# Joined SwiGLU products of 512 columns, a reordered beginning, and moved weight splits in a two-block transformer kernel

## The reference

```python
def swiglu(x, w13, w2):
    g, u = jnp.split(x @ w13, 2, axis=-1)
    return (jax.nn.silu(g) * u) @ w2
...
        if kind == 0:
            mix = gated_deltanet(h, a_w_in[j], a_conv[j], a_a_log[j], a_dt_bias[j], a_norm_g[j], a_w_out[j])
        elif kind == 1:
            mix = moba_attention(h, b_w_qkv[j], b_w_out[j])
...
        h = layer_norm(DEEPNORM_ALPHA * h + mix, ln1_g[i], ln1_b[i])
        h = layer_norm(DEEPNORM_ALPHA * h + swiglu(h, f_w13[i], f_w2[i]), ln2_g[i], ln2_b[i])
...
def half_ffn(h, shift, scale, gate, g_pre, g_post, w13, w2):
    u = modulate(rmsnorm(h, g_pre), shift, scale)
    return h + 0.5 * gate * rmsnorm(swiglu_2(u, w13, w2), g_post)
```

## Time and profile before

| | before |
|---|---|
| three timed runs | 1744.97, 1747.71 (median), 1751.12 us |
| profiled execution, its own time | 1749.66 us |
| its span | 1747.9 us |
| mean granted TensorE clock | 0.984 |
| busy share PE, PEld, DVE, ACT, POOL | 96%, 88%, 54%, 44%, 9% |
| read from HBM | 303.69 MB, 174 GB/s over the span |

### The profile page before, as it was taken

How to read it: one execution, slowest core, us unless ns; L and a number is a source line. 1 busy time by engine, 2 the same in 40 slices (tenths; PEclk the granted TensorE clock), 3 DMA queues, 4 the chain that set the end, 5 groups by cost and what they waited for, 6 DMA issues and landing times.

```text
span 1747.9 us, 27671 instructions
## 1 busy us (share of the span) xinstructions
PE 1680.7 (96%) x11886; PEld 1539.4 (88%) x11886; DVE 948.0 (54%) x1085; ACT 764.5 (44%) x979; POOL 165.4 (9%) x170
## 2 busy tenths in 40 slices
PE   7999999999899899999999999999999999989998
PEld 6996787999777689988999899989889999879997
DVE  4664236554535565556655565556766364665543
ACT  4454333444325534433444354444655354444432
POOL 0113420000000100001000130012100020020000
PEclk8999999999999999999999999999999999999999
DMA  7553238665556786655765566645445242676652
GB/s 230 146 180 133 98 121 252 183 191 186 202 175 235 243 248 188 189 193 169 196 179 184 180 191 174 188 169 183 154 141 154 69 138 92 199 224 180 177 187 95
DMA packets 329168, 306.54 MB, mean 175 GB/s; under 512 B 11953, under 2 KB 286934, under 8 KB 328918
## 3 DMA queue, kind: packets, MB, share of 16 engines
q1 hardware_dynamic: 324246, 296.19, 55.3%
q10 hardware_dynamic: 4528, 7.54, 1.3%
q0 software_dynamic: 272, 1.05, 0.2%
HBM read 303.69 MB, written 1.05 MB: 174 GB/s over the span
## 4 chain that ended last, share of the span: by engine, by line
PE 87%; DVE 6%; ACT 3%; DMA 2%; issue 1%; POOL 1%; SPq 0%; DVEq 0%; POOLq 0%; ACTq 0%
PE ps L412 49%; PE ps L436 17%; PE ps L455 8%; ACT whi L383 2%; PE ps L473 1%; DVE wlo L389 1%; PE ps L1178 1%; PE ps L1194 1%; PE ps L1798 1%; PE ps L594 1%; DMA raw<-in_b_w_qkv 1%; PE ps L2396 1%; PE ps L2295 1%; DVE x L708 1%; DVE small L663 0%
## 5 line engine op out<-in xcount | busy, mean ns | idle before, releaser
L389 DVE TENSOR_TENSOR wlo<-raw,whi 128x2048 fp32r<-128x2048 f32 x247 | 567.7, 2300 | 408.6 <-ACT whi L383 408.5
L412 PE MATMUL ps<-ah,whi 128*128 128x256 f32 x2368 | 678.1, 286 | 7.1 <-DVE wlo L389 7.1
L412 PE MATMUL ps<-ah,wlo 128*128 128x256 f32 x2368 | 672.8, 284 | 0.0
L412 PE MATMUL ps<-al,whi 128*128 128x256 f32 x2368 | 672.8, 284 | 0.0
L383 ACT CAST whi<-raw 128x2048 fp32r<-128x2048 f32 x247 | 470.0, 1905 | 246.6 <-PE ps L436 157.1
L412 PEld LDWEIGHTS ps<-ah,whi 128*128 128x128 f32 x2368 | 457.5, 193 | 10.1 <-issue 7.1
L412 PEld LDWEIGHTS ps<-al,whi 128*128 128x128 f32 x2368 | 457.4, 193 | 1.8 <-issue 1.4
L412 PEld LDWEIGHTS ps<-ah,wlo 128*128 128x128 f32 x2368 | 457.2, 193 | 0.0
L764 ACT ACTIVATE f_sig<-ps 128x256 f32<-128x256 f32 x110 | 42.1, 383 | 359.2 <-PE ps L412 345.3
L436 PE MATMUL ps<-whi,fh 128*128 128x512 f32 x440 | 171.6, 390 | 0.0
L436 PE MATMUL ps<-wlo,fh 128*128 128x512 f32 x440 | 171.3, 389 | 0.0
(11 more groups left out here) (360 smaller groups left out, 1642.2 us busy)
## 6 DMA issues: line engine op xcount, KB each, us to landing
raw<-in_f_w SPq DMA_DIRECT2D x132, 512.0 KB, 4.6
raw<-in_w_a SPq DMA_DIRECT2D x132, 512.0 KB, 4.6
raw<-in_w_ada SPq DMA_DIRECT2D x72, 512.0 KB, 4.6
raw<-in_w_in SPq DMA_DIRECT2D x68, 512.0 KB, 4.6
raw<-in_w_b SPq DMA_DIRECT2D x66, 512.0 KB, 4.7
raw<-in_a_w_in SPq DMA_DIRECT2D x32, 512.0 KB, 5.2
raw<-in_b_w_qkv SPq DMA_DIRECT2D x24, 512.0 KB, 5.8
raw<-in_a_w_out SPq DMA_DIRECT2D x8, 512.0 KB, 4.0
```

The lines of the kernel that those rows point to most:

```text
L389: dve.tensor_tensor(wlo[:, c % RING, :], raw[:, r % RING, :], whi[:, c % RING, :].bitcast(F32), ALU.subtract).then_inc(S("lo_ready"), 1)
L412: last = pe.matmul(out_ap, a, b, start=(i == 0), stop=(i == n - 1))
```

## The change

It does four things.

1. The up segments become kind "U". For each block and `k` there is one product of 512 columns, wh x [ah | al] (`ah` and `al` are now the two halves of one tile `a_split`), and one of 256, wl x ah. The sums xh·wh + xh·wl stand in the left half of a bank and xl·wh in the right half; a chunk takes two banks. ACT copies both right halves out, DVE adds them to the left halves, and Silu and the product follow (`gate_sum`, `summed`).
2. At the beginning the two tiles of x are loaded first on two queues, the turn goes in the order 0, 2, 1, 3, chunk 0 is split in two halves, PE gets six products of a constant around the turn (`warm_pe`), the gates are computed as 16 rows (24 products of 256 columns, a copy and two transposes), `params_pe` moves from behind chunk 0 to behind chunk 1, and the sums and norms move two chunks later.
3. On DVE, the splits of up0's, m_qkv's, up1's and up4's chunk 1 move from in front of the row pass to behind the turn (turns 1, 2, 3 and 8).
4. The row pass in front of up2 is spread over DVE's work on up2's chunks 0 to 3.

```diff
-        Segment("up0", KF, "B", gate_up(A["f_w13"][0]), evicted="hid"),
+        Segment("up0", KF, "U", gate_up(A["f_w13"][0]), evicted="summed"),
...
+    UP_BANKS = ((0, 1), (2, 4), (5, 6))
...
+        sp.dma_start(x0[:, 1, :], A["x"][0, P:T, :]).then_inc(S("x_in1"), 16)
...
+    def start_cuts_act(act):
+        act.wait_ge(*S("landed0", 32))
+        act.copy(whi[:, 0, 0:HALF], raw[:, 0, 0:HALF]).then_inc(S("hi_first"), 1)
+        act.copy(whi[:, 0, HALF:CHUNK], raw[:, 0, HALF:CHUNK]).then_inc(S("hi_ready"), 1)
+        for c in range(1, RING):
+            cut_hi(act, c)
+    def start_cuts_dve(dve):
+        for name, done, half in (("hi_first", "lo_first", slice(0, HALF)), ("hi_ready", "lo_ready", slice(HALF, CHUNK))):
+            dve.wait_ge(*S(name, 1))
+            dve.tensor_tensor(wlo[:, 0, half], raw[:, 0, half], whi[:, 0, half].bitcast(F32), ALU.subtract)\
+               .then_inc(S(done), 1)
+        cut_lo(dve, 1)
+        small_weight_cut(dve)
+        cut_lo(dve, 2)
...
+    def up_products(pe, q, j, slot, f, ks):
+        wh, wl = (p[:, slot, :].rearrange("p (k n) -> p k n", k=KD) for p in (whi, wlo))
+        o, cols_ = ps[q.bank[j][f]], slice(f * P, f * P + P)
+        for k in ks:
+            if k == KD - 1:
+                pe.matmul(o[:, 0:T], wl[:, k, cols_], ah[:, k, :], start=False, stop=False)
+            last = pe.matmul(o[:, :].rearrange("p (s t) -> p s t", s=2), wh[:, k, cols_], a_split[:, :, k, :],
+                             start=(k == 0), stop=(k == KD - 1))
+            if k < KD - 1:
+                pe.matmul(o[:, 0:T], wl[:, k, cols_], ah[:, k, :], start=False, stop=False)
+        return last
...
+            if n == 2 and j in (1, 2):
+                pe.wait_ge(*S("ln_sum", 12 + (1, 3)[j - 1]))
+            if n == 3 and j in (1, 2):
+                pe.wait_ge(*S("res_scaled", (1, 3)[j - 1]))
...
+                    if k == tt == h == 0:
+                        pe.wait_ge(*evicted("up" + name[4:], KF - 2))
...
+        act.dma_start(x0[:, 0, :], A["x"][0, 0:P, :]).then_inc(S("x_in0"), 16)
         act.dma_start(table[:, 0:P], A["table"][:, 0:P]).then_inc(S("ident_in"), 16)
-        for tt in range(TT):
-            act.dma_start(x0[:, tt, :], A["x"][0, tt * P:tt * P + P, :]).then_inc(S(f"x_in{tt}"), 16)
...
+    def warm_pe(pe, bank_):
+        pe.wait_ge(*S("warm_set", 1))
+        for _ in range(3):
+            pe.matmul(ps[bank_][:, :], warm[:, 0:P], warm[:, :], start=True, stop=True)
...
+    def turn_order(n):
+        return (0, 2, 1, 3) if n == 0 else range(4)
...
         cut_ahead(dve, q.cut[1])
-        cut_ahead(dve, q.cut[2])
         if n == 0:
             ada_sum_dve(dve, 2)
...
-            act.activation(f_sig[:, j % RING, :], ps[b][:, 0:T], ACT.Silu).then_inc(S("silu"), 1)
+            wait_from(act, *S("hid", j + (KF * n - RING + 1)))
+            act.copy(f_sig[:, j % RING, :], ps[b[0]][:, T:2 * T]).then_inc(S("low_sums"), 1)
+            wait_from(act, *S("hid_lo", j + (KF * n - RING + 1)))
+            act.copy(f_act[:, j % RING, :], ps[b[1]][:, T:2 * T]).then_inc(S("low_sums"), 1)
             if j:
                 hi(j - 1)
+            act.wait_ge(*S("gate_sum", j + (KF * n + 1)))
+            act.activation(f_sig[:, j % RING, :], f_sig[:, j % RING, :], ACT.Silu).then_inc(S("silu"), 1)
             cut_ahead(act, c)
...
-            dve.wait_ge(*S("silu", j + (KF * n + 1)))
-            wait_from(dve, *S("hid_lo", j + (KF * n - RING + 1)))
-            dve.tensor_tensor(f_act[:, j % RING, :], ps[b][:, T:2 * T], f_sig[:, j % RING, :], ALU.mult)\
-               .then_inc(S("hid"), 1)
+            i, sig, act_ = j + KF * n, f_sig[:, j % RING, :], f_act[:, j % RING, :]
+            dve.wait_ge(*S("low_sums", 2 * i + 1))
+            dve.tensor_tensor(sig, ps[b[0]][:, 0:T], sig, ALU.add).then_inc(S("gate_sum"), 1)
+            dve.wait_ge(*S("low_sums", 2 * i + 2))
+            dve.tensor_tensor(act_, ps[b[1]][:, 0:T], act_, ALU.add).then_inc(S("summed"), 1)
+            dve.wait_ge(*S("summed", i + 1))
+            dve.wait_ge(*S("silu", i + 1))
+            dve.tensor_tensor(act_, act_, sig, ALU.mult).then_inc(S("hid"), 1)
             if j:
                 lo(j - 1)
             cut_ahead(dve, c)
@@ -801,7 +885,7 @@
         lo(KF - 1)
         def down(j, c, b):
-            if n or j < KF // 2 - 1:
+            if n or j < KF // 2 - 2:
...
+        pairs = []
+        for k in range(KD):
+            pairs += [(swh[:, k, :], ah[:, k, :]), (swh[:, k, :], al[:, k, :]), (swl[:, k, :], ah[:, k, :])]
+        products(pe, ps[7][0:16, 256:512], pairs).then_inc(S("gate_rows_ps"), 1)
...
             if j == 0:
+                gates_pe(pe)
+            if j == 1:
                 params_pe(pe)
-                gates_pe(pe)
+                gates_turn_pe(pe)
             if j == 2:
+                pe.wait_ge(*S("cols_ready", 4))
+            if j == 4:
+                pe.wait_ge(*S("tables_in", 16))
...
+            if 4 <= j < 12:
+                pe.wait_ge(*S("squares", j - 3))
...
         cut_ahead(dve, q.cut[3])
-        for j in range(3):
+        for j in range(2):
...
+        warm_pe(pe, 7)
         turn_pe(pe, 0, x0)
+        warm_pe(pe, 3)
...
         ln_rows(dve, 0)
         turn_dve(dve, 1)
+        cut_ahead(dve, segs["g_out"].cut[2])
         cut_ahead(dve, segs["g_out"].cut[3])
         ffn_dve(dve, 0)
         ln_sums_of_down(dve, 1, segs["down0"])
         ln_rows(dve, 1)
         turn_dve(dve, 2)
+        cut_ahead(dve, segs["down0"].cut[KF // 2 - 2])
         ada_sum_dve(dve, 3)
         cut_ahead(dve, segs["down0"].cut[KF // 2 - 1])
...
+        cut_ahead(dve, segs["m_out"].cut[2])
         cut_ahead(dve, segs["m_out"].cut[3])
...
-        ln_rows(dve, 3)
         def second_rows_dve(e, j):
-            if j != UP_AT:
-                return
-            rms_dve(e, 1, x0)
+            if j < 4:
+                ln_rows(e, 3, [j])
+            if j == UP_AT:
...
         turn_dve(dve, 8, mod_scale(4))
+        cut_ahead(dve, segs["w_out"].cut[2])
         cut_ahead(dve, segs["w_out"].cut[3])
```

More of the change, by code:

```diff
@@ L301, in build @@
         Segment("w_out", 4, "A2", halves(A["w_out_2"][0])),
-        Segment("up4", KF, "B", gate_up(A["w13_b_2"][0]), evicted="hid"),
+        Segment("up4", KF, "U", gate_up(A["w13_b_2"][0]), evicted="summed"),
         Segment("down4", KF // 2, "W2", rows(A["w2_b_2"][0])),
@@ L413, in products, with up_pe, body @@
         return last
+    def up_products(pe, q, j, slot, f, ks):
[9 more added lines that the diff above has]
+        return last
+    def up_pe(pe, n, more, turn=None):
+        q = segs[f"up{n}"]
+        def body(j, c, b):
+            pe.wait_ge(*S("lo_ready", c + 1))
+            bank_free(pe, q, j)
+            if n == 2 and j in (1, 2):
+                pe.wait_ge(*S("ln_sum", 12 + (1, 3)[j - 1]))
+            if n == 3 and j in (1, 2):
+                pe.wait_ge(*S("res_scaled", (1, 3)[j - 1]))
+            if turn and j == 0:
+                for kh in range(2):
+                    pe.wait_ge(*S("act_lo", 4 * turn + kh + 3))
+                    for f in range(2):
+                        last = up_products(pe, q, j, c % RING, f, range(4 * kh, 4 * kh + 4))
+            else:
+                for f in range(2):
+                    last = up_products(pe, q, j, c % RING, f, range(KD))
+            last.then_inc(S("used"), 1)
+            more(j)
+        walk(q, body)
     def stream_pe(pe, name, xh, xl, more=lambda j: None, turn=None, only=None, ready=lambda j, tt: None):
@@ L602, in turn_act @@
     def turn_act(act, n, last_of=None):
-        for b in range(4):
+        for i, b in enumerate(turn_order(n)):
             if n > 3:
@@ L631, in turn_dve @@
         if n < 4:
-            for b in range(4):
-                lo(b)
+            for i, b in enumerate(turn_order(n)):
+                lo(b, i)
             return
@@ L904, in more @@
                 last.then_inc(S("norms_ps"), 1)
-        stream_pe(pe, "g_qkv", ah, al, more)
+        stream_pe(pe, "g_qkv", ah, al, more, turn=0)
         stream_pe(pe, "g_z", ah, al)
```

100 lines of the change are left out of this document (54 added, 46 removed).

## The result

The changed kernel takes 1754.99 us (median of 20 runs, 1751.21 to 1758.58) against 1747.68 (median of 20, 1744.68 to 1756.11). The ratio is 1.0031, with a 95% interval from 1.0019 to 1.0043: it is slower by 0.3%, and the whole interval lies above 1. The profiled execution has a span of 1753.6 us, 5.7 more than before. (The medians are 7.3 apart; the profiled execution of the kernel before lies 2 us above its median.)

The account below looks back on a forecast made before the run. PE's stream was taken to bound the kernel, with DVE and ACT hidden inside it. Terms -23.2 + 1.8 - 4.8 - 2.8 + 33.2 + 3.5 = +7.7 on 1747.7 gave 1755.4, called 1755 us; range 1738 to 1770.

Parts of the forecast that it names:

- Joined products: Up products: one 512-column and one 256-column product replace three of 256, saving 0.21 us a chunk in 110 chunks, -23.2 us.
- second rival: Up products: a joined product takes as long as two narrow ones (0.2400), so no saving and 1779 us; chance 0.10.
- Row pass of up2: Spreading it ends a 2.3 us wait but makes later splits 4.1 us late in all: +1.8 us.
- The beginning: Start to g_qkv's chunk 4: PE starts earlier at 12.9, but a new wait holds chunk 4 until 45.6: -4.8 us.
- Turn 2: Turn before m_qkv: without the split in front, the norm begins at 474.9 instead of 477.70, -2.8 us.
- Turns 1, 3 and 8: Before up0, up1, up4: ada loads wait for the moved splits, and PE for their landing; +10.0, +10.0, +13.2, together +33.2 us.
- Clock: After 10 us of idle each at turns 1, 3 and 8, PE runs at half clock for a while: +3.5 us.
- late load hidden: Turns 1, 3 and 8: ada load not held by the split or landing inside the turn, 1717 us; chance 0.13.
- Joining saves little: Up products: joined product takes as long as two narrow ones, so the -23.2 is lost and 1779 us; chance 0.10.
- No wait at chunk 4 and landings at their lower bound: Beginning -9, turns +29, clock +1, no lateness in up2: about no change, 1741 to 1746 us; chance 0.20.

Follow-up runs that it names:

- experiment 3: Changed kernel with the high and low half of each k side by side, so a joined product streams one piece: 1755.9 us, ratio 1.0029.
- experiment 5: Changed kernel with each block's products reordered to one wide, eight narrow, then seven wide: 1753.7 us, ratio 1.0021 to the kernel before.
- experiment 11: Changed kernel without the six constant products around turn 0: 1761.7 us, ratio 1.0064 to the kernel before.
- experiment 4: Changed kernel with the parameter transposes behind chunk 0's gate products again instead of behind chunk 1: 1752.4 us, ratio 1.0012 to the kernel before.
- experiment 7: Kernel before with only the splits of up0's, up1's and up4's chunk 1 moved behind turns 1, 3 and 8: 1782.0 us, ratio 1.0188.
- experiment 12: Kernel before with only the joined up products and their evictions added: 1737.9 us, ratio 0.9924.
- experiment 6: Changed kernel with m_qkv's chunk 1 split in front of the row pass of turn 2 again: 1757.1 us, ratio 1.0047 to the kernel before.
- experiment 2: Changed kernel with PE multiplying ada 14, 30, 34 and 35 behind up's chunk 0 instead of in front: 1739.3 us, ratio 0.993 to the kernel before.

## Why the prediction was right, and where it was not

The forecast was 1755 and 1755.0 was measured. Its mechanism at the turns, which decides the sign, was that of the trace. That the number came out to the microsecond is luck: two terms are off by 10 and 6 us, two waits and one gain were not in the sum at all, and the errors cancel. In the order of the prediction:

- **Joined products, -23.2.** This term was mis-sized. The wide product was priced as one of down's, 0.2268, and takes 0.2355, the narrow one 0.1170: 1760 x 0.0075 = -13.2. The 5.64 us a chunk lie between the forecast's 5.55 and the 5.76 of the second rival (its sign was given as 5.74; 16 x 0.36 is 5.76). Neither the layout (experiment 3) nor wholly the change of width (experiment 5) explains it. The 4.4 us that the prediction worked out from the fixed cost in the Trainium skill (page "TensorE: Matmul & The Clock Gate", section "Wait — 56ns, not 53.3ns?") are no better: too small by 8.8, where the rows' 23.2 were too large by 10.0. The evictions were hidden, as said. The joined form's new wait at up3's chunk 1 was put at nothing; with the slow restart behind it, it costs 0.9.
- **Row pass of up2, +1.8.** The lateness is there, in front of chunks 6, 7 and 9 (the split of the last stands behind the RMS pass of body 5), with 0.35, 0.35 and 1.2 us of idle; DVE's body took 6.2 us and not 6.5, and PE's chunk 5.64 and not 5.55. Start to start these lose 2.4, what the wait at chunk 3 lost before: up2 gained 2.5 us, and the joined rate alone gives 2.6, so this term is +0.1. The 0.5 for GpSimd beside DVE came from no row, and no run shows it.
- **The beginning, -4.8.** -6.5 to the end of ada 13. The new wait at chunk 4 was there, 4.3 us start to start where 5 were forecast, ended by DVE's split as said. The start came at 11.9, 1 us sooner than estimated, and chunk 0 took 5.8 us and kept none of the excess over 5.76: that excess was half clock, which the constant products took over (experiment 11). That the parameter copies cause the wait is only half true (experiment 4). The -6.5 is one execution's: in the six traces that have the same beginning, the last product of ada 13 starts at 267.4 to 270.6 us, with 3 to 14 us at half clock before it.
- **Turn 2, -2.8.** PE's gap fell by 2.76. Another 2.8 went in m_qkv, where two idle stretches of before (2.0 and 1.7 start to start) are missing. This is no effect of the change that any run shows: such stretches stand in the kernel before, in experiment 7 and again in experiment 11, which has the joined products and the moved split; they are missing in experiment 12, which has only the joined products, and in experiment 6, which has the split back. What the three profiles with them share is the landing: the loads of w_qkv issued behind an ada load (but for the first, right behind the turn) land 7.2 to 8.2 us after their issue, and 6.6 to 7.1 in the other eleven. Why they land later is open.
- **Turns 1, 3 and 8, +33.2.** +8.0, +8.3 and +10.5, together 26.8. The chain was right step by step: split behind the low halves, issue behind the split, landing, ada products. The mis-sized step is the landing, 5.0 us where 6.7 were taken and 7.6 where 9.4 were. The chunks issued behind the load did not slow it. The 6.5 us of the row from which the 6.7 came was no matter of other ada chunks, as ada 13 had landed when that load was issued; but between 274.4 and 281.5 a second DMA queue (q10 of the profile) took 26% of the engines' time, and 7% between 280.6 and 285.7 in the changed kernel. That this is the reason is not shown.
- **Clock, +3.5.** Half clock lasts 2.7 us into up0, 2.7 into up1 and 3.4 into up4, before 0.6, 1.6 and none; half of the difference is +3.3.

The terms as measured: -13.2 + 0.9 + 0.1 - 6.5 - 5.6 + 26.8 + 3.3 = +5.8. With +0.4 from down3 to ada 33, where the second new wait of 1.0 us lies, this is 6.2, where the spans differ by 5.7. But 2.8 of it are the stretches in m_qkv, and the beginning and the mLSTM part vary by 3 and 5 us from one execution to the next, so the agreement of a single pair of traces is partly luck too.

Of the rivals, *late load hidden* fell: it would have shown no idle. *Joining saves little* is half true in its size and wrong in its sign of the total, since experiment 12 is a gain. *No wait at chunk 4 and landings at their lower bound* was right on the landings and wrong on the wait.

## What to carry to other kernels

Before a step is moved behind another, look at what it releases: here a split that was needed late itself was also the release of a buffer, and so of a load on an in-order queue that PE needed early. When such a load is late, changing who waits for it moves the wait (experiment 2), and putting the release back removes it. A sum that comes out right can hide terms that are 20 to 40% off; single-part runs such as 7 and 12 show it. And look for what a new form holds on to: a chunk with two banks instead of one waited in two places for banks that others still used.
